# The 31-tap convolution's running sums in two PSUM banks, with the stage's matmuls on the six others

## What is computed

```python
def conv_module(a, g, conv_w, conv_b, ln_g, ln_b, w_co, b_co):
    u = a * jax.nn.sigmoid(g)
    u = lax.conv_general_dilated(
        u, conv_w[:, None, :].astype(u.dtype), window_strides=(1,),
        padding=[(CONV_WIDTH - 1, 0)],
        dimension_numbers=("NWC", "WIO", "NWC"),
        feature_group_count=CONV_DIM) + conv_b
    u = jax.nn.silu(layer_norm(u, ln_g, ln_b))
    return u @ w_co + b_co
...
    h = x @ w_in[l] + b_in[l]
    conv_a, conv_g, q, k, v, r, f_lr, gate_a, gate_b = jnp.split(h, split_points, axis=-1)
    y_conv = conv_module(conv_a, conv_g, conv_w[l], conv_b[l], conv_ln_g[l], conv_ln_b[l],
                         w_conv_out[l], b_conv_out[l])
    y_gla = gla_branch(q, k, v, r, f_lr, w_gate_up[l], b_gate_up[l], gla_norm_g[l], w_gla_out[l])
```

## Time and profile before

| | us |
|---|---|
| median of 3 runs | 1941.87 |
| lowest and highest | 1939.96, 1944.76 |
| the profiled execution | 1940.17 |
| its span, first to last instruction | 1938.4 |

### The profile page before, as it was taken

One profiled execution on the slowest core, in us unless ns is written; L12 is line 12 of the kernel. 1 busy time (PEld: TensorE's weight loads), 2 busy tenths in 40 slices (PEclk: granted clock), 3 DMA queues, 4 the chain that ended last, 5 costly groups with the idle time before them and its releaser, 6 DMA issues.

```text
span 1938.4 us, 21397 instructions
## 1 busy us (share of the span) xinstructions
PE 1451.7 (75%) x9194; PEld 998.4 (52%) x9194; DVE 625.4 (32%) x870; ACT 451.6 (23%) x554; POOL 613.0 (32%) x151
## 2 busy tenths in 40 slices
PE   7856687896667656666567766765699878899897
PEld 6756587761233212322132312331499868799885
DVE  1999755520000000000000000000574962247702
ACT  3322334210000000000000000000446635444433
POOL 6855936400000000000000000000465756597782
PEclk9978898988889888998899888888699989899999
DMA  8322322779999999999999999999445434354440
GB/s 318 141 87 91 125 98 111 271 285 409 409 409 410 410 410 410 410 410 410 409 410 410 410 410 410 410 410 409 189 156 185 160 109 161 125 193 175 174 174 22
DMA packets 116576, 539.42 MB, mean 278 GB/s; under 512 B 4440, under 2 KB 8544, under 8 KB 108832
## 3 DMA queue, kind: packets, MB, share of 16 engines
q1 hardware_dynamic: 113232, 532.44, 70.4%
q0 software_dynamic: 1184, 3.94, 0.6%
q10 hardware_dynamic: 2096, 2.11, 0.4%
HBM read 537.41 MB, written 1.06 MB: 278 GB/s over the span
## 4 chain that ended last, share of the span: by engine, by line
DMA 37%; PE 27%; DVE 14%; SPq 6%; ACT 5%; issue 3%; POOL 3%; DVEq 0%; ACTq 0%
DMA ring<-in_w 36%; PE bank L527 19%; SPq L361 6%; PE bank L746 5%; DVE slab L1377 3%; DVE slab L1373 3%; POOL ring_parts L465 3%; ACT ring_parts L988 2%; DMA ring<-in_units 1%; PE bank L732 1%; DVE slab L1460 1%; DVE rows_parts L1707 1%; DVE slab L1801 0%; DVE slab L1438 0%; PE bank L781 0%
## 5 line engine op out<-in xcount | busy, mean ns | idle before, releaser
L465 POOL TENSOR_TENSOR ring_parts<-ring,ring_parts 128x2048 fp32r<-128x2048 f32 x114 | 594.2, 5238 | 283.8 <-ACT ring_parts L988 283.7
L527 PE MATMUL bank<-slab_parts,ring_parts 128*128 128x256 f32 x3328 | 513.9, 291 | 73.6 <-POOL ring_parts L465 23.1
L746 PE MATMUL bank<-ring,slab 128*32 128x512 f32 x2016 | 336.6, 801 | 290.7 <-DMA ring<-in_w 289.5
L527 PEld LDWEIGHTS bank<-slab_parts,ring_parts 128*128 128x128 f32 x3328 | 472.1, 199 | 80.4 <-POOL ring_parts L465 24.4
L746 PEld LDWEIGHTS bank<-ring,slab 128*32 128x32 f32 x2016 | 66.6, 125 | 559.8 <-DMA ring<-in_w 381.0
L479 POOL TENSOR_TENSOR slab_parts<-slab,slab_parts 128x1088 fp32r<-128x1088 f32 x1 | 2.5, 2491 | 945.1 <-ACT slab_parts L1137 945.1
L988 ACT ACTIVATE ring_parts<-ring 128x2048 fp32r<-128x2048 f32 x114 | 211.5, 1908 | 111.2 <-PE bank L527 110.7
L1641 DVE TENSOR_TENSOR slab<-slab,bank 128x512 f32<-128x512 f32 x16 | 11.0, 688 | 611.1 <-PE bank L746 611.1
L1377 DVE SCALAR_TENSOR_TENSOR slab<-slab,cols 128x254 f32<-128x254 f32 (+23 forms) x312 | 193.1, 697 | 0.1
L527 PE MATMUL bank<-ring_parts,slab_parts 128*128 128x512 f32 (+1 forms) x672 | 169.1, 403 | 28.3 <-DVE slab L1359 13.4
L527 PE MATMUL bank<-rows_parts,ring_parts 128*128 128x256 f32 x752 | 187.2, 286 | 0.0
(11 more groups left out here) (286 smaller groups left out, 906.1 us busy)
## 6 DMA issues: line engine op xcount, KB each, us to landing
ring<-in_w SPq DMA_DIRECT2D x190, 2048.0 KB, 23.7
ring<-in_units SPq DMA_DIRECT2D x59, 2048.0 KB, 7.9
slab<-in_w SPq DMA_DIRECT2D x2, 2048.0 KB, 14.6
ring<-in_units SPq DMA_DIRECT2D x2, 1024.0 KB, 14.0
slab<-bias_scratch ACTq DMA_DIRECT2D x2, 1024.0 KB, 8.0
slab<-in_xT SPq DMA_DIRECT2D x1, 1024.0 KB, 5.1
rows<-in_ln_g POOLq DMA_DIRECT2D x2, 512.0 KB, 9.0
slab<-in_x SPq DMA_DIRECT2D x1, 1024.0 KB, 5.0
```

The lines of the kernel that those rows point to most:

```text
L465: g.tensor_tensor(r32(w), w, r32(high), ALU.subtract).then_inc(S("low_ready"), 1)
L527: return mm(out_, l, r, start=start and first, stop=stop and last)
L746: last = mm(b[CAP * j:CAP * j + CAP, :], xg[:, c, CAP * j:CAP * j + CAP], wt[:, j, i, :], start=c == 0, stop=c == DC - 1, tile_position=(0 ...
```

## The change

The running sums of the convolution move from slab to PSUM. `long_conv` replaces `causal_conv` for this convolution: each half keeps its four sums in the halves of banks 6 and 7, lag 0 writes them, lags 1 to 29 read and write them, and lag 30 reads them and writes `chan(3)` in slab, which it does for the tokens from 30 on; two copies a half bring the first 30 tokens over, so `conv_tap` counts two more a half. `causal_conv` stays for the second block's shorter convolutions. Up to csum the other tasks take turns on banks 0 to 5 (`_bank_table`); from csum on banks 6 and 7 join in, first in the row, and all eight take turns.

```diff
-TASK = {name: i for i, name in enumerate(TASKS1 + TASKS2)}
+FEW = 6
+
+
+def _bank_table():
+
+
+    table, uses, turn_ = {}, [0] * 8, list(range(FEW))
+    for name in TASKS1 + TASKS2:
+        b = turn_.pop(0)
+        turn_.append(b)
+        table[name] = (b, uses[b])
+        uses[b] += 1
+        if name == "csum":
+            turn_ = list(range(FEW, 8)) + turn_
+    return table
+
+
+BANK = _bank_table()
...
         def take_bank(task):
 
-            if TASK[task] >= 8:
-                nc.tensor.wait_ge(S(f"bank_read{TASK[task] % 8}"), TASK[task] // 8)
+            b, use = BANK[task]
+            if use:
+                nc.tensor.wait_ge(S(f"bank_read{b}"), use)
             return bank(task)
...
                 if c % 4 == 0:
-                    pe.wait_ge(S("conv_tap"), 4 * CONV_W * (c // 4 + 1))
+                    pe.wait_ge(S("conv_tap"), (4 * CONV_W + 2) * (c // 4 + 1))
...
+            def long_conv(half_, base, between):
+
+
+                src, dst, done = chan(2), chan(3), "conv_tap"
+                sums = [banks[FEW + i // 2][:, T * (i % 2):T * (i % 2) + T] for i in range(4)]
+                chunks = range(4 * half_, 4 * half_ + 4)
+                n = 0
+                for lag in range(CONV_W):
+                    j = CONV_W - 1 - lag
+                    for c, sum_ in zip(chunks, sums):
+                        wc = col("conv_w", CONV_W * c + j)
+                        if lag == 0:
+                            ins = ts(sum_, src[:, c, :], wc, col("conv_b", c), ALU.mult, ALU.add)
+                        else:
+                            dve.wait_ge(S(done), base + n - 3)
+                            out_ = dst[:, c, lag:T] if lag == CONV_W - 1 else sum_[:, lag:T]
+                            ins = stt(out_, src[:, c, 0:T - lag], wc, sum_[:, lag:T], ALU.mult, ALU.add)
+                        ins.then_inc(S(done), 1)
+                        n += 1
+                    if lag in between:
+                        between[lag]()
+                for i in range(2):
+                    c = 4 * half_ + 2 * i
+                    v.tensor_copy(dst[:, c:c + 2, 0:CONV_W - 1],
+                                  banks[FEW + i][:].rearrange("p (m t) -> p m t", m=2)[:, :, 0:CONV_W - 1]
+                                  ).then_inc(S(done), 1)
+                    n += 1
+                dve.wait_ge(S(done), base + n)
+                return base + n
...
-            n = causal_conv(chan(2), chan(3), "conv_w", CONV_W, "conv_b", [(c, c, c) for c in range(4)],
-                            "conv_tap", 0, between={GLU_LAG: lambda: glu_input([2, 3]), GATE_LAG: gate_negabs})
+            n = long_conv(0, 0, {GLU_LAG: lambda: glu_input([2, 3]), GATE_LAG: gate_negabs})
...
-            causal_conv(chan(2), chan(3), "conv_w", CONV_W, "conv_b", [(c, c, c) for c in range(4, 8)],
-                        "conv_tap", n, between={V_LAGS[0]: lambda: take_v(0), V_LAGS[1]: lambda: take_v(1)})
+            long_conv(1, n, {V_LAGS[0]: lambda: take_v(0), V_LAGS[1]: lambda: take_v(1)})
```

More of the change, by code:

```diff
@@ L220, in build @@
         hT = slab[:, 1:4, :].rearrange("p a (c t) -> p (a c) t", c=DC)
-        turn_ = [banks[(TASK["pos"] + 1 + i) % 8] for i in range(8)]
+        turn_ = [banks[BANK[name][0]] for name in TASKS1[-8:]]
         acc = [turn_[0:2], turn_[2:4]]
@@ L240, in bank @@
         def bank(task):
-            return banks[TASK[task] % 8]
+            return banks[BANK[task][0]]
         def take_bank(task):
-            if TASK[task] >= 8:
-                nc.tensor.wait_ge(S(f"bank_read{TASK[task] % 8}"), TASK[task] // 8)
+            b, use = BANK[task]
+            if use:
+                nc.tensor.wait_ge(S(f"bank_read{b}"), use)
             return bank(task)
         def full(ins, task):
-            ins.then_inc(S(f"bank_full{TASK[task] % 8}"), 1)
+            ins.then_inc(S(f"bank_full{BANK[task][0]}"), 1)
         def wait_full(eng, task):
-            eng.wait_ge(S(f"bank_full{TASK[task] % 8}"), TASK[task] // 8 + 1)
+            b, use = BANK[task]
+            eng.wait_ge(S(f"bank_full{b}"), use + 1)
             return bank(task)
         def read(ins, task):
-            ins.then_inc(S(f"bank_read{TASK[task] % 8}"), 1)
+            ins.then_inc(S(f"bank_read{BANK[task][0]}"), 1)
         def wait_read(eng, *tasks):
             for task in tasks:
-                eng.wait_ge(S(f"bank_read{TASK[task] % 8}"), TASK[task] // 8 + 1)
+                b, use = BANK[task]
+                eng.wait_ge(S(f"bank_read{b}"), use + 1)
         def home(n):
```

## The result

The kernel after takes 1866.86 us in the median (four runs, 1866.17 to 1870.79), the kernel before 1940.91 beside it (four runs, 1939.84 to 1944.76). The ratio is 0.9618, with a 95% interval of 0.9606 to 0.963. The profiled execution of after has a span of 1864.4 us; its listing's lines stand some 20 further down than the same lines before, and those behind `long_conv` some 50 (a tap is L1400, lag 0 L1396, GpSimd's low part L485, a product L547, csum L658). Mind one number that changes its meaning: L1008 is ScalarE's high part now, and the gate's exponential is L1028.

A forecast was written before the change was run, and what follows sets the result against it. VectorE and GpSimd taking turns on SBUF, with TensorE waiting, was taken as the bound. Waits 61.6 plus lower clock 10.4 less 0.6 gave 71.4 us: 1940.17 to 1868.8 profiled, plus 1.7 makes 1870.5; range 1860 to 1900.

The forecast's parts named there:

- What bounds: Convolution stage, 44 to 240 us: VectorE and GpSimd take turns reading SBUF, and TensorE stands still 61.6 us.
- The taps: The convolution's 240 taps: with sums in a bank, no turns with GpSimd and 0.39 us each; bounds 0.39 and 0.65.
- a fixed bit: Rival at the taps: a write to a bank costs 0.08 us more each, 13.8 us, giving 1884; chance 0.13.
- two passes: Rival at the taps: reading and writing a bank take a pass each, 0.26 us more a tap, 1926; chance 0.07.
- the slower one: Rival at the taps: in-place sum in a bank takes 0.72 us or more, so csum waits for them; chance 0.04.
- Lag 0: First tap of each half, eight instructions writing a bank: 1.6 us for four, instead of 12.50 and 18.57.
- The rival at 1881 to 1898: Lag 0 still takes turns with GpSimd, and r2 waits 10.9 up to 17.0 us longer; chance 0.07.
- VectorE's times: VectorE's queue in the convolution: second half's lag 0 at 106.9 us, that half's end at 157.5.
- TensorE's times: TensorE from v to csum: v 21.8 us, the 480 matmuls 58.3, csum at 164.2 instead of 235.61.
- r2's wait of 0.6: TensorE's r2 takes v1_0's bank, wanted at 128.6 and free at 129.2: one wait of 0.6 us.
- Behind csum: Everything after csum keeps its order and moves as a block; VectorE's and GpSimd's turns there stay as they are.
- given back behind csum: Rival: turns fall otherwise after csum and return some 10 to 25 us, 1880 to 1895; chance 0.04.

The follow-up runs named there:

- the run with v1 read later: Changed kernel with VectorE's read of the v1 tasks behind lag 20 of the second half instead of lag 12; 1882.51 us, ratio 0.9682.
- the six banks alone: Changed kernel's bank table with both halves' convolution sums back in slab, run against the kernel before; 1943.68 us, ratio 0.9998.
- the run with the memset: Kernel before, with GpSimd's low-part subtraction replaced by a one-column memset for units up to gb1; 1869.78 us, ratio 0.9619.
- the kernel with the mean in a bank: Changed kernel with csum's mean scaled and kept in csum's own bank for the eight centering subtractions; 1865.41 us, ratio 0.9594.

## Why the prediction was right

The forecast of 1870.5 is 3.6 us above the median measured; the profiled execution was put at 1868.8 and took 1866.17. The mechanism and the sum for the stage came out; that the terms' errors nearly cancel, in the stage and behind it, is luck. By the steps:

**What bounds.** VectorE and GpSimd taking turns, with TensorE the one who waits. Taking VectorE's second SBUF read away, or GpSimd's reads, gives nearly the same time, 1867.24 and 1869.78, and csum at 163.3 and 163.8. The 40.1 us of ScalarE's wait went with the rest, as it was said to be a consequence. Two readings of the prediction are off and carry nothing: VectorE is at nine tenths in slices 2 to 4 and at seven in slice 5, with 5, 5, 5 and 2 behind it (and at nine once more in slice 32), and GpSimd's piece of 195.48 began 2.8 us into the 72 taps from 192.71, so it sat through the rest of them.

**The taps.** 0.39 a tap was taken for the read and the write of a bank; the 72 of 44.58 are (27.57 less the last one's 0.48) / 71 = 0.38 apart. The unknown, whether a write to the bank costs a pass or a fixed bit, came out at nothing. With the read in the bank and the write in slab, 27.56 us: the same to 0.01. The rivals of a fixed bit (1884), of two passes (1926) and the slower one (above 0.72 a tap) fall by this row. The 65 ns that the Trainium skill's page "VectorE: DVE Perf Modes", section on the TRN2 errata, would add for a PSUM source aren't there, neither in the spacing nor in the length of a record (0.48 us for 255 columns in after, 0.47 with both operands in slab and GpSimd not reading).

**Lag 0.** 1.6 was taken, 1.89 measured, 0.45 a piece where a tap has 0.38. It doesn't take its turn with GpSimd's group of 36.32 to 54.71, which ran all around it. The rival at 1881 to 1898 falls, and this agrees with what the prediction cites the Trainium skill for at this step.

**VectorE's times.** Lag 0 of the second half at 104.98 (106.9 was said), the half's end at 154.55 (157.5). Of these three microseconds 1.2 are the earlier start, 0.7 come up to lag 0 of the second half and 1.0 in it, since a tap is 0.38 rather than 0.39. The wait at L1458 behind a GpSimd piece came (2.50 us for 1.2).

**TensorE's times.** v took 23.5 us, from 82.30 to 105.80, where 21.8 was said. The working took the full clock for all of v, and the trace of after has 0.57 in 82 to 86 us, and 1.00 from there to 163:

```profile
82.00:86.00 4.00, 4.00 (x11) 2.96 (x10) 4.00 (x13) 3.98 (x7) 3.81 (x1) 0.57 0.26 111
86.00:106.00 20.00, 20.00 (x90) 16.53 (x90) 18.05 (x25) 7.64 (x6) 13.56 (x4) 1.00 0.30 105
```

Four microseconds at 0.57 do the work of 2.3, which is the 1.7 that are missing. Before had 1.00 in these same 4 us; why after hasn't isn't shown. The 480 matmuls took 57.6 (58.3 was said). 1.7 too little for v, 0.7 and 0.6 too much for the products and the wait and 1.2 for the start nearly cancel, by luck: csum at 163.39, where 164.2 was said. r2's wait of 0.6 didn't come, since v1_0's bank was free at 127.1 and wanted near 128.9; the run with v1 read later shows that this bound was the next to bite.

**Behind csum.** The block was to move as a whole, with VectorE's and GpSimd's turns as they were. It did move as a whole: TensorE's lead over before is 72.2 us at csum, 73.1 at 191 us, 70.9 at 308, 73.7 at 326, 74 to 76 in the experts' stage and 74.0 at the end. But its inside changed twice. First, the turns did not stay. One of VectorE's steps that reads slab twice, before and then after:

```profile
311.13 3.26 DVE L1469 SCALAR_TENSOR_TENSOR slab<-slab,cols 128x256 f32<-128x256 f32 x8
```

```profile
238.02 7.63 DVE L1517 SCALAR_TENSOR_TENSOR slab<-slab,cols 128x256 f32<-128x256 f32 x8
```

A GpSimd piece that began at 240.52 fell on it, where before the next one came only at 314.07. That costs 4.4 us, and a step further on gives 2.3 back (L1388 took 4.61 us, L1438 takes 2.29). This is the rival "given back behind csum", with 2 us in place of its 10 to 25. Second, the clock. The second 16 routing matmuls and the eight behind them ran at 0.50 before and run at 1.00 in after:

```profile
387.38 3.66 PE L704 MATMUL bank<-w_route,slab 128*128 128x72 f32 x16 [0.78 <-ACT slab L1086]
```

```profile
315.92 1.98 PE L724 MATMUL bank<-w_route,slab 128*128 128x72 f32 x16 [0.83 <-ACT slab L1106]
```

With the steps around them this gives 2.7 us of lead. The prediction had neither. So the 74.0 are 71.0 from the stage, 1.2 from ahead of it, 0.8 from the clock in gb0 (13.08 us for 13.85), 2.2 lost to the turns, 2.7 won by the clock in the routing and half a microsecond not traced further.

One thing was missing in the reasoning, though it cost the prediction nothing: that a change of waits re-arranges others. By the same reasoning the six banks alone were expected to cost 8 us or more, and they cost nothing that the times can show.

## What to carry to other kernels

Where VectorE is slow beside a busy GpSimd, count its operands in SBUF. Here a VectorE instruction with two of them exchanged turns with GpSimd's instructions that read SBUF, and moving one of the two to PSUM cost nothing and ended it for both engines. Making the other engine's instructions shorter was no substitute: a row of back-to-back taps held some of the short ones as long as the long ones. Before an edit is priced by the waits that it adds, ask whether these keep the colliding engine off; and when a block moves, ask which collisions inside it move too.

## What the runs showed of the hardware

- A running sum kept in a PSUM bank, read and written by the same VectorE instruction, costs what one in SBUF does: 0.38 us from one 255-wide tap to the next, against 0.39.
- A TENSOR_SCALAR from SBUF to a bank, 256 wide, takes 0.45 us from one to the next with GpSimd reading all around it. The same from SBUF to SBUF takes part in the turns, 12.51 us for four, and 1.38 for four without GpSimd (the run with the memset, at 43.16).
- The turns aren't shared out evenly, and what shares them out isn't known. In the kernel before, GpSimd's pieces from 57.15 and 68.00 got through a row of taps at once, with one tap let in after each piece of 4.6 to 4.9 us, while those of 83.37 and 195.48 waited for the end of the taps in front of VectorE's next other step. With pieces of 1.3 us three got through at once and others waited up to 19 us.
- TensorE's granted clock at one place of the program differs between kernels that are alike there: the second 16 routing matmuls ran at 1.00 (1.98 us) in two of the traces and at 0.50 (3.66 us) in the others. In the kernel with the mean in a bank this took 4.4 us of a 6.4 us gain. What decides it is open.
